# Heads' scores in three visits of TensorE a step instead of five, with operands in second buffers

## What is computed

```python
def step(state, inp):
    qc, kc, vc, gc = inp
    bcum = jnp.cumsum(gc, axis=2)
    o_inter = jnp.einsum("bhtd,bhde->bhte", qc * jnp.exp(bcum), state)
    rel = jnp.where(tri, bcum[:, :, :, None, :] - bcum[:, :, None, :, :], 0.0)
    decay = jnp.where(tri, jnp.exp(rel), 0.0)
    scores = jnp.einsum("bhtd,bhsd,bhtsd->bhts", qc, kc, decay)
    o_intra = jnp.einsum("bhts,bhse->bhte", scores, vc)
    b_end = bcum[:, :, -1:, :]
    state = state * jnp.exp(b_end)[:, :, 0, :, None] + jnp.einsum(
        "bhsd,bhse->bhde", kc * jnp.exp(b_end - bcum), vc)
    return state, o_inter + o_intra
```

## Time and profile before

| | us |
|---|---|
| median of 3 runs (lowest, highest) | 2220.19 (2214.09, 2221.35) |
| the profiled execution | 2222.61 |
| its span, first to last instruction | 2220.8 |
| PE busy / DVE busy in the span | 2119.3 / 1531.7 |

### The profile page before, as it was taken

The page is one execution under the profiler, slowest core; times in us unless marked ns, Lnnn a source line. Parts: engine busy times, 40 slices in busy tenths (PEclk is TensorE's granted clock), DMA queues, the critical chain, the costliest instruction groups (busy, mean ns, idle before and its releaser), DMA issues.

```text
span 2220.8 us, 48212 instructions
## 1 busy us (share of the span) xinstructions
PE 2119.3 (95%) x20564; PEld 1780.2 (80%) x20564; DVE 1531.7 (69%) x3275; ACT 508.6 (23%) x836; POOL 74.5 (3%) x109
## 2 busy tenths in 40 slices
PE   5799999999999999999999999999996989999997
PEld 2799988788788888888887888787775777888886
DVE  5865854126878877787878787789886776555564
ACT  3711133101111211111121112111113343212121
POOL 0001101000000000000000000000000000000000
PEclk9999999999999999999999999999997999999999
DMA  8444554332324333334243343432434457544451
GB/s 313 158 136 144 182 154 152 119 131 84 118 85 139 96 118 104 121 99 129 82 124 104 91 133 96 127 111 92 127 104 155 157 190 246 183 140 152 156 175 57
DMA packets 229863, 298.89 MB, mean 135 GB/s; under 512 B 14934, under 2 KB 159990, under 8 KB 226322
## 3 DMA queue, kind: packets, MB, share of 16 engines
q1 hardware_dynamic: 145346, 178.38, 24.8%
q10 hardware_dynamic: 73952, 81.18, 10.8%
q0 software_dynamic: 10352, 36.25, 5.0%
HBM read 198.16 MB, written 97.59 MB: 133 GB/s over the span
## 4 chain that ended last, share of the span: by engine, by line
PE 88%; DVE 5%; DMA 2%; issue 2%; ACT 1%; SPq 1%; ACTq 0%; DVEq 0%
PE all_bank L61 25%; PE all_bank L63 24%; PE all_bank L62 23%; PE all_bank L1479 3%; PE all_bank L1469 2%; PE all_bank L1423 2%; PE all_bank L1439 2%; PE all_bank L1452 1%; PE all_bank L1462 1%; PE all_bank L1478 1%; DVE hidden_h_lo L483 1%; DMA front_w_mod<-in_w_ada 1%; SPq L366 1%; PE all_bank L1008 1%; PE all_bank L2563 1%
## 5 line engine op out<-in xcount | busy, mean ns | idle before, releaser
L61 PE MATMUL all_bank<-hidden_h_hi,head_hi 128*128 128x512 f32 x1184 | 491.0, 415 | 1.6 <-issue 1.6
L63 PE MATMUL all_bank<-hidden_h_hi,head_lo 128*128 128x512 f32 x1184 | 465.7, 393 | 0.0
L62 PE MATMUL all_bank<-hidden_h_lo,head_hi 128*128 128x512 f32 x1184 | 463.2, 391 | 0.0
L1515 ACT ACTIVATE head_projected<-all_bank 128x512 f32<-128x512 f32 x148 | 88.4, 597 | 865.3 <-PE all_bank L63 865.3
L63 PEld LDWEIGHTS all_bank<-hidden_h_hi,head_lo 128*128 128x128 f32 x1184 | 222.7, 188 | 51.8
L61 PEld LDWEIGHTS all_bank<-hidden_h_hi,head_hi 128*128 128x128 f32 x1184 | 222.8, 188 | 47.0 <-issue 2.1
L62 PEld LDWEIGHTS all_bank<-hidden_h_lo,head_hi 128*128 128x128 f32 x1184 | 223.3, 189 | 41.2 <-issue 1.5
L1615 DVE RECIPROCAL head_inverse<-head_gate 128x448 f32<-128x448 f32 x64 | 185.9, 2932 | 0.0
L1666 DVE TENSOR_TENSOR head_query<-head_query,head_total 128x256 f32<-128x256 f32 x256 | 108.4, 424 | 81.5 <-PE all_bank L1439 51.8
L61 PE MATMUL all_bank<-front_hi,hidden_h_hi 128*128 128x256 f32 x512 | 143.6, 281 | 0.0
L63 PE MATMUL all_bank<-front_hi,hidden_h_lo 128*128 128x256 f32 x512 | 142.5, 278 | 0.0
(11 more groups left out here) (294 smaller groups left out, 4161.2 us busy)
## 6 DMA issues: line engine op xcount, KB each, us to landing
head_raw<-in_w_in POOLq DMA_DIRECT2D x37, 512.0 KB, 4.9
head_value<-value_rows SPq DMA_DIRECT2D x64, 256.0 KB, 5.1
head_query<-piece_query SPq DMA_DIRECT2D x64, 256.0 KB, 6.7
head_out<-head_o ACTq DMA_DIRECT2D x64, 256.0 KB, 6.1
tail_o<-head_out SPq DMA_DIRECT2D x32, 512.0 KB, 6.0
front_raw<-in_w_in SPq DMA_DIRECT2D x19, 512.0 KB, 5.1
front_stage<-in_x SPq DMA_DIRECT2D x16, 512.0 KB, 6.6
front_w_mod<-in_w_ada SPq DMA_DIRECT2D x8, 1024.0 KB, 13.7
```

The source lines that it names most:

```text
L61: nc.tensor.matmul(out, st_hi, mv_hi, start=start, stop=False)
L62: nc.tensor.matmul(out, st_hi, mv_lo, start=False, stop=False)
L63: return nc.tensor.matmul(out, st_lo, mv_hi, start=False, stop=stop)
L1515: nc.scalar.activation(projected[unit % 2][:], ps_proj[unit % 2][:], PIECES[name][1], scale=PIECES[name][2]).then_inc(proj_copied, 1)
```

## The change

`query` and `key` have one buffer per direction, not two. Beside them each direction has `query_planes` and `key_planes`, two planes of 512 columns each: plane "far" holds the operands of levels 8, 16 and 32 and at last those of the output and the transposes; plane "turned" gets those of level 64. The product of a level into PSUM is issued by `level_in_parts` for levels 8 and 16, with the same operands' shapes as before. `far_operands` (the multiplication that stood at the head of a step, behind its near product) runs at the end of the step before, from `query`/`key` into "far". `next_level(n, d, 2)` writes half of "turned" without waiting for level 32's product; level 64 then multiplies a mixture of both planes (`joint_query`, `joint_key`), blocks of 32 columns, with 32 columns of keys and 64 of queries at a time: 16 products in place of 8. Before the transposes four small copies on ACT (`returned`) bring the mixed blocks back into "far". SP may load `query` and `key` of the next step only when this step's near products are done and its "far" operands are written. The first head's second load, which was issued ahead in the front, goes the same way.

```diff
-    query = [[piece(f"query{d}{b}", at + d * row) for b, at in enumerate((VALUES + 6 * row, RAW))] for d in range(2)]
-    key = [[piece(f"key{d}{b}", at + d * row) for b, at in enumerate((HC + 6 * row, RAW + 2 * row))] for d in range(2)]
+    query = [piece(f"query{d}", VALUES + (6 + d) * row) for d in range(2)]
+    key = [piece(f"key{d}", HC + (6 + d) * row) for d in range(2)]
+    PLANES_AT = (RAW, spare + 3 * row)
+    two_planes = lambda n, offset: r.at(n, [P, 2, GRP], offset)
+    query_planes = [two_planes(f"query_planes{d}", PLANES_AT[d] + d * row) for d in range(2)]
+    key_planes = [two_planes(f"key_planes{d}", PLANES_AT[d] + (1 - d) * row) for d in range(2)]
+    query_far = [query_planes[d][:, d, :] for d in range(2)]
+    key_far = [key_planes[d][:, 1 - d, :] for d in range(2)]
+    query_turned = [query_planes[d][:, 1 - d, :] for d in range(2)]
+    key_turned = [key_planes[d][:, d, :] for d in range(2)]
...
+    def joint(planes, side):
+
+        return planes[:].rearrange("p a (n two c) -> p n a two c", two=2, c=32)[:, :, :, side, :]
+
+    def blocks_of_32(ap):
+
+        return ap.rearrange("p (n a c) -> p n a c", a=2, c=32)
+
+    def joint_query(d):
+
+        return joint(query_planes[d], d)
+
+    def joint_key(d):
+
+        return joint(key_planes[d], 1 - d)
...
-                    wait_count(sp, product[d], PROD * (NG * h + g))
+                    wait_count(sp, product[d], PROD * (NG * h + g) + 1)
+                    wait_count(sp, operand[d], OPS * (NG * h + g) + 2)
...
-            project_half(h, g, 1)
-            project_half(h, g, 2)
             if n == 0:
                 pe.wait_ge(handed.evacuated, handed.all_fills)
-            for i in range(2):
-                for d in range(2):
-                    wait_count(pe, operand[d], OPS * n + 2 + i)
-                    if i == 0:
-                        wait_count(pe, chained[d], CHAIN * n)
-                    else:
...
-            for i, size in ((2, 32), (3, 64)):
-                for d in range(2):
-                    wait_count(pe, operand[d], OPS * n + 2 + i)
...
+            level_in_parts(n, 0)
+            for slot in range(1, 3):
+                project_half(h, g, slot)
+            level_in_parts(n, 1)
+            for slot in range(3, 5):
+                project_half(h, g, slot)
+            for d in range(2):
+                wait_count(pe, operand[d], OPS * n + 4)
+            for t in range(TPG):
+                for pair in range(2):
+                    for d in range(2):
+                        s, q = (2 * pair, 2 * pair + 1) if d == 0 else (2 * pair + 1, 2 * pair)
+                        done = nc.tensor.matmul(ps[d][2][PARTS[s], t, PARTS[q]], tile(key_far[d], t)[:, PARTS[s]], tile(query_far[d], t)[:, PARTS[q]],
+                                                start=True, stop=True)
+                        if t == TPG - 1 and pair == 1:
+                            done.then_inc(product[d], 1)
+            for d in range(2):
+                wait_count(pe, operand[d], OPS * n + 5)
+            for t in range(TPG):
+                for side in range(2):
+                    for d in range(2):
+                        done = nc.tensor.matmul(ps[d][2][PARTS[2 * d + side], t, (1 - d) * 64:(2 - d) * 64], joint_key(d)[:, 2 * t + d, side, :],
+                                                joint_query(d)[:, 2 * t + 1 - d, :, :], start=True, stop=True)
+                        if t == TPG - 1 and side == 1:
+                            done.then_inc(product[d], 1)
+            for slot in range(5, 8):
+                project_half(h, g, slot)
             for d in range(2):
                 wait_count(pe, operand[d], OPS * n + OPS)
                 wait_count(pe, copied[d], MASKED * n + 1)
+                wait_count(pe, returned[d], 2 * (n + 1))
...
-            for slot in range(9):
+            for slot in range(5):
+                evacuate(h, g, slot)
+            for d in range(2):
+                wait_count(act, product[d], PROD * n + 5)
+                for into, turned, two in ((key_far[d], joint_key(d), 1 - d), (query_far[d], joint_query(d), d)):
+                    a = 1 - two
+                    into, turned = (ap.rearrange("p (n two) a c -> p n two a c", two=2)[:, :, two, a, :] for ap in (blocks_of_32(into), turned))
+                    nc.scalar.activation(into, turned, ACT.Copy).then_inc(returned[d], 1)
+            for slot in range(5, 9):
...
+        def far_operands(h, g):
+            n = NG * h + g
+            for d in range(2):
+                qs, ks, q_far, k_far, f = (in_blocks(ap, d) for ap in (query[d][:], key[d][:], query_far[d], key_far[d], gate[d][:]))
+                wait_count(v, product[d], PROD * n)
+                wait_count(v, operand[d], OPS * n + 1)
+                nc.vector.tensor_tensor(q_far, qs, f[:, :, 0:1].to_broadcast([P, GRP // BASE, BASE]), ALU.mult)
+                nc.vector.tensor_tensor(k_far, ks, f[:, :, BASE - 1:BASE].to_broadcast([P, GRP // BASE, BASE]), ALU.mult
+                                        ).then_inc(operand[d], 1)
+                wait_count(v, chained[d], CHAIN * n)
+                wait_count(v, copied[d], MASKED * n)
+                nc.vector.tensor_tensor(total_of(d, BASE), f[:, :, 0], f[:, :, BASE - 1], ALU.mult).then_inc(totalled[d], 1)
+
+        def next_level(n, d, i):
+            size = LEVELS[i]
+            tot = total_of(d, size).rearrange("p (n two o) -> p n two o", two=2, o=1)
+            shape = [P, GRP // (2 * size), size]
+            if i != 2:
+                wait_count(v, product[d], PROD * n + 2 + i)
+            wait_count(v, operand[d], OPS * n + 2 + i)
+            wait_count(v, totalled[d], TOT * n + 1 + i)
+            if i < 2:
+                qs, ks = ordered(query_far[d], d, size)[:, :, 1, :], ordered(key_far[d], d, size)[:, :, 0, :]
+                nc.vector.tensor_tensor(qs, qs, tot[:, :, 0, :].to_broadcast(shape), ALU.mult)
+                nc.vector.tensor_tensor(ks, ks, tot[:, :, 1, :].to_broadcast(shape), ALU.mult).then_inc(operand[d], 1)
+            elif i == 2:
+                qs, ks = ordered(query_far[d], d, size), ordered(key_far[d], d, size)
+                q_into, k_into = ordered(query_turned[d], d, size), ordered(key_turned[d], d, size)
+                nc.vector.tensor_tensor(q_into[:, :, 0, :], qs[:, :, 1, :], tot[:, :, 0, :].to_broadcast(shape), ALU.mult)
+                nc.vector.tensor_tensor(k_into[:, :, 1, :], ks[:, :, 0, :], tot[:, :, 1, :].to_broadcast(shape), ALU.mult
+                                        ).then_inc(operand[d], 1)
+            else:
+                qs, ks = ordered_joint(joint_query(d), d)[:, :, 1, :, :], ordered_joint(joint_key(d), d)[:, :, 0, :, :]
+                q_into, k_into = ordered_joint(blocks_of_32(query_far[d]), d)[:, :, 1, :, :], ordered_joint(blocks_of_32(key_far[d]), d)[:, :, 0, :, :]
+                tot_q, tot_k = (tot[:, :, j, :].rearrange("p n (a o) -> p n a o", a=1).to_broadcast([P, TPG, 2, 32]) for j in range(2))
+                nc.vector.tensor_tensor(q_into, qs, tot_q, ALU.mult)
+                nc.vector.tensor_tensor(k_into, ks, tot_k, ALU.mult).then_inc(operand[d], 1)
+            wait_count(v, copied[d], MASKED * n + min(i, MASKED - 1))
+            nc.vector.tensor_tensor(total_of(d, 2 * size), tot[:, :, 0, 0], tot[:, :, 1, 0], ALU.mult).then_inc(totalled[d], 1)
...
+            def prepare_next(level, parts):
+                due = split_due(h, g, level)
+                if not ends:
+                    prepare(*next_step(h, g), parts[0])
+                if due is not None:
+                    split_low(h, due)
+                if not ends:
+                    prepare(*next_step(h, g), parts[1])
+
+            for d in range(2):
+                next_level(n, d, 0)
...
+            prepare_next(1, (0, 1))
+            for i in (1, 2):
                 for d in range(2):
...
+                    next_level(n, d, i)
+            prepare_next(2, (2, 3))
+            prepare_next(3, (4, 5))
+            for d in range(2):
+                next_level(n, d, 3)
+            prepare_next(4, (6, 7))
...
                 first_operands(*next_step(h, g))
+                far_operands(*next_step(h, g))
```

101 lines of the change are left out of this document (36 added, 65 removed).

## The result

| | before | after |
|---|---|---|
| median of 4 runs, us | 2220.77 (2214.09 to 2222.46) | 2298.02 (2296.21 to 2300.99) |
| the profiled execution's span | 2220.8 | 2299.2 |
| PE busy | 2119.3 | 2143.4 |

The ratio is 1.0358, with a 95% interval of 1.0332 to 1.0383: slower by 77 us. The sign was forecast, the size was not: 2256 was the figure, and 2298 lies 6 us above the upper end of the range.

The account below looks back on a forecast made before the run. PE was taken to bound the heads stage. Gains 19.6 + 3 + 9.4 = 32 us against losses 63 + 5 = 68 brought the profiled 2222.6 to 2259, 2256 as median; range 2215 to 2292.

Parts of the forecast that it names:

- two visits fewer: On PE, joining near with level 8 and level 32 with level 64 saves 0.63 us a step, 19.6 us.
- stops in the burst: Joined near and level 8: PE waits 2.3 us for instructions in twelve ten-slot steps (27.6 us), where two block edges fall.
- wait for the loads: PE waits at level 64 for DVE, held by later loads: 8.8 us in twelve ten-slot steps, 26.8 in seven eight-slot.
- `far` operands: On DVE, 2.8 us moved to the end of a step: costs nothing, though without its cover up to 1 us a step.
- clock: Pauses of 2 to 4 us in some 19 steps bring PE's clock down 3 to 4 times, 1.6 us each: 5 us.
- last step: Without projections there, two PE waits for operands go and two round trips shrink: gain of 3 us, ends 1 and 5.
- as once in four now: Rate at which PE's pauses bring the clock down, from the earlier kernel's four pauses; one low-clock period worth 1.6 us.
- the 8.8 of the sum: The next step's loads land 8.8 us after SP's first issue, between 7.9 at least and 10.6 at most.
- rival 1: Only the loads are late, PE's instructions keep up: losses 46.6 us and 2 for the clock, 2236 us; chance 0.25.
- The thin cover: PE's outputs and slot 0 hide DVE's moved operands, done 0.3 to 1 us before level 8 asks: no cost.
- The fixed cost of a visit: PE going over to a level's products and back costs 0.31 to 0.32 us, beside the records themselves.
- The four stops of before: Inside or behind level 8's visit PE waits for instruction fetches, 7.8 us; they go or become new waits, 9.4 with clock.

Follow-up runs that it names:

- one edge and no load wait: Changed kernel with next step's preparation behind levels 32 and 64's operands, and level 16's first products repeated so each joined visit holds one block edge: 2213.7 us.
- the two kernels that differ in 31 products: Changed kernel, preparation later, level 16's first products repeated; 31 extra products in the first step put two block edges in joined visits: 2320.5 us, without them 2213.7.
- one edge only: Changed kernel with level 16's first products repeated 4 to 24 more a step, one block edge in every joined visit, preparation not moved: 2299.9 us.
- the kernel with the later preparation: Changed kernel with DVE's first two parts of the next step's preparation moved behind the operands of levels 32 and 64: 2248.9 us.
- the kernel with two edges: Changed kernel, preparation later, level 16's first products repeated, 31 of them in the first step, so every joined visit holds two block edges: 2320.5 us.

## Why the prediction missed, step by step

From the near scores of the first step to those of the last the heads stage grew by 81.5 us. Intervals from start to start divide it so; the last two rows bring it to the whole span, 78.4:

| us | predicted | measured |
|---|---|---|
| two visits fewer | -19.6 | -13.3 |
| stops in the burst, less those of before (7.8) | +19.8 | +27.6 |
| wait for the loads, levels 32 and 64 | +35.6 | +33.7 |
| `far` operands | 0 | +4.4 |
| clock, less that of before | +3.4 | +29.1 |
| last step (and tail) | -3 | -4.6 |
| the stage begins later | 0 | +1.5 |
| sum | +36 | +78 |

Of the -4.6, the last step itself has 2.3; the rest lies in the tail, which the change does not touch.

- **The step that failed is the price of the clock.** The stops and the waits were forecast in kind, place and nearly in size. But "as once in four now" made 5 us of half-clock time for 19 steps with stops of 2 to 4 us (one in four of 19 would have been 7.6 at 1.6 each; the sum took 3 to 4 stretches). Here 14 of 15 stops and six double waits each brought a stretch, at some 1.5 us, and 26 of the 42 us of the miss are this term. It is counted from intervals; no run takes the low clock away and leaves the stops. With one edge and no load wait it is 1.6 us, so that the stops and waits are what calls it up, not the small products. The rate of one in four came from four stops, and the range took no account of it being four in four.
- **The burst was read right.** Two edges within it stop PE, and it was half of the steps: 15 of 31. One stop was put at 2.3 us; the three lines marked issue make 33.0 / 15 = 2.2. The 8 us by which the term was short are mostly their number: the sum had twelve. Twelve lie in ten-slot steps of heads 1, 3 and 5, as many as were counted, the other three in the first step and in two with eight slots. That the stops come from the place of the edges is shown by the two kernels that differ in 31 products.
- **The Trainium skill** (Runtime: NRT & Kernel Launch, Instruction fetch mechanics) says that an edge is mostly hidden. The trace agrees for one edge in the burst (of the 30 steps made so, none stops) and disagrees for two (all 30 steps made so stop, and 15 of 16 in the changed kernel). Its room of 2048 instructions for PE is not what these runs show: 384 records in a row were enough to stop it.
- **The loads** landed as I took it. In the steps shown the second key began 9.0 and 9.85 us behind the first issue, but over the 31 groups of six loads of the changed kernel the last landed 8.9 us behind the first issue in the median (7.8 to 10.4), against the 8.8 of the sum; before it was 10.2. The 35.6 was near for the wrong reason in part: where no stop covers it, the wait is 60.1 us (one edge only, 57.9 without the last step), not the 46.6 of rival 1, whose world measured 2300, 6 of them repeats, not 2236. I had PE wait at level 64 alone; it waits at level 32 too, for DVE makes the two levels' operands one behind the other.
- **The thin cover was named and given nothing.** The `far` operands hold PE 0.9 us in steps that begin a head, where DVE has a split to do as well. Waits below 0.6 us of the same kind are in the -13.3, and so are 2 us of level 64's products at the low clock. Level 64's new form costs nothing: 0.60 us from its first start to that of L61, where it was 0.61.
- **The fixed cost of a visit** held where nothing waits. PE around the joined visit in the step of 1204.27:

```profile
1203.94 0.40 PE L63 MATMUL all_bank<-hidden_h_hi,head_lo 128*128 128x512 f32 x1
...
1205.55 0.73 PE L1452 MATMUL all_bank<-head_query_planes,head_key_planes 128*32 128x16 f32 x63
1206.21 0.50 PE L61 MATMUL all_bank<-hidden_h_hi,head_hi 128*128 128x512 f32 x1
1206.55 0.39 PE L62 MATMUL all_bank<-hidden_h_lo,head_hi 128*128 128x512 f32 x1
```

  From L63 to L62 2.61 us. In the earlier trace rows the near visit took 2.05 in that measure (L63 at 1008.92, L61 at 1010.63 and L62 0.34 behind it) and level 8's 1.33, less the 0.46 that stands there anyway: 2.92. That is the forecast 0.31.
- **The four stops of before** were said to come from fetches held up by the loads. They go when the loads are issued later, and nothing else is changed: that they need the loads beside them is shown. That it is a fetch that the loads hold up is argued from their place, at block edges like the others.
- **Order of the causes.** Taking the wait for the loads away gives 49 us, taking the burst or its stops away 12 or nothing, both 81 to 84. A decomposition of one trace adds up, its terms do not come off one by one.

What stays open: why 14 of 15 stops halved the clock here, while the same 15 did so nine times in the kernel with the later preparation, the four before only once, and the 33 in the kernel with two edges 24 times. Stops of 1.9 us stand on both sides.

## What to carry to other kernels

Giving up a second buffer moves a load behind its reader; the price is not the load but whatever stands behind its wait on the engine in order, so move the waiting instruction back with it: that alone gave 49 us here, clock included. A gain from merging visits of short instructions is to be set against the instruction stream, since a burst that spans two block edges waits for its instructions. And price a stop of PE with the slow clock that may follow it, here 1.5 us on top of 2, behind 14 of 15 stops in one kernel and 9 of 15 in another; a rate taken from four stops is not to be relied on. Two causes that cover each other have to be taken away together: taking the stops away gave nothing by itself, and 35 us once the wait for the loads was gone.

## What the runs showed of the hardware

- PE's stops lie 256 PE and PEld records apart or a multiple of it, PE's waits counted too, in every kernel here; one instruction packet holds 16.4 KB. 384 records in 1.9 us with two such edges stop PE, 2.2 us on average and 3.4 at most in the waits (15 of 16 steps by chance, all 30 made so); with one edge they did not stop it in any step before the last.
- A stop or a pair of waits of 2 us and more was followed by the 1.2 GHz level in many cases (14 of 15 stops, 9 of 15, 24 of 33, 1 of 4 in four kernels), seen as projections 0.43 us apart for some 3 us.
- Products of 32 key and 64 query columns, two records each, start 31 ns apart on average (32 records in 0.49 us) when they go over four groups of 32 columns in turn, and 0.1 us apart when one product is repeated in one group.
- Six loads of 256 KB, issued in 3 us from one queue, are in at 8.9 us behind the first issue in the median of 31 steps (7.8 to 10.4), 1.3 us sooner than with the output stores beside them (10.2 before).
